# Two transformer blocks in float32 on one core: more tile pairs by seven block products, later waits, and subtractions moved from GpSimd to VectorE

## The reference

```python
def swiglu_ffn(h, w13, w2):
    g, u = jnp.split(h @ w13, 2, axis=-1)
    return (jax.nn.silu(g) * u) @ w2
```

## Time and profile before

| what | value |
|---|---|
| median of 3 runs | 1855.22 us (1853.93 to 1859.35) |
| the profiled execution's own time | 1851.81 us |
| its span in the profile | 1849.7 us |
| mean granted clock of TensorE | 0.996 of full speed |

### The profile page before, as it was taken

One profiled execution on the slowest core, in us unless ns is written; L12 is line 12 of the kernel. 1 busy time (PEld: TensorE's weight loads), 2 busy tenths in 40 slices (PEclk: granted clock), 3 DMA queues, 4 the chain that ended last, 5 costly groups with the idle time before them and its releaser, 6 DMA issues.

```text
span 1849.7 us, 28967 instructions
## 1 busy us (share of the span) xinstructions
PE 1811.9 (98%) x10711; PEld 1496.1 (81%) x10711; DVE 1076.8 (58%) x1548; ACT 764.8 (41%) x1137; POOL 217.5 (12%) x178
## 2 busy tenths in 40 slices
PE   7999999999999999999999999999999999999998
PEld 6787776788888888888879998788776879998787
DVE  6553686466777533444677777334666477776322
ACT  6635436454444322322443335223555353334322
POOL 0030001111111100000300003401000200003510
PEclk9999999999999999999999999999999999999999
DMA  6312112133333333333323333333220223333331
GB/s 192 82 37 58 47 47 69 46 92 99 94 101 92 94 94 100 100 96 98 95 88 102 91 102 99 94 94 105 77 77 1 80 81 101 102 91 105 90 104 66
DMA packets 309232, 161.08 MB, mean 87 GB/s; under 512 B 12688, under 2 KB 306832, under 8 KB 309024
## 3 DMA queue, kind: packets, MB, share of 16 engines
q1 hardware_dynamic: 308080, 157.28, 29.2%
q0 software_dynamic: 640, 2.17, 0.4%
q10 hardware_dynamic: 432, 0.52, 0.1%
HBM read 157.85 MB, written 2.10 MB: 86 GB/s over the span
## 4 chain that ended last, share of the span: by engine, by line
PE 91%; POOL 4%; DVE 2%; ACT 2%; issue 1%; DMA 0%; ACTq 0%; DVEq 0%
PE ps L382 27%; PE ps L384 27%; PE ps L383 27%; POOL h_hi L859 4%; PE ps L2116 1%; PE ps L1527 1%; PE ps L2433 1%; PE ps L2434 1%; PE ps L2107 1%; PE ps L1438 1%; PE ps L1844 1%; PE ps L1260 1%; PE ps L1788 1%; PE ps L1832 0%; PE ps L2213 0%
## 5 line engine op out<-in xcount | busy, mean ns | idle before, releaser
L382 PE MATMUL ps<-xhi,whi 128*128 128x512 f32 (+1 forms) x1512 | 584.5, 387 | 8.1 <-DVE t_lo L785 6.1
L383 PE MATMUL ps<-xlo,whi 128*128 128x512 f32 (+1 forms) x1512 | 575.4, 381 | 0.0
L384 PE MATMUL ps<-xhi,wlo 128*128 128x512 f32 (+1 forms) x1512 | 575.1, 380 | 0.0
L369 ACT ACTIVATE whi<-raw 128x1024 fp32r<-128x1024 f32 (+2 forms) x297 | 308.3, 1038 | 578.8 <-PE ps L384 578.3
L377 DVE TENSOR_TENSOR wlo<-raw,whi 128x1024 fp32r<-128x1024 f32 (+2 forms) x279 | 350.4, 1256 | 237.6 <-ACT whi L369 237.5
L382 PEld LDWEIGHTS ps<-xhi,whi 128*128 128x128 f32 x1512 | 285.4, 189 | 67.0 <-issue 11.3
L383 PEld LDWEIGHTS ps<-xlo,whi 128*128 128x128 f32 x1512 | 285.6, 189 | 54.9 <-issue 3.1
L384 PEld LDWEIGHTS ps<-xhi,wlo 128*128 128x128 f32 x1512 | 285.5, 189 | 54.6
L382 PE MATMUL ps<-h_lo,whi 128*128 128x512 f32 x352 | 137.4, 390 | 1.6 <-POOL h_hi L859 1.6
L384 PE MATMUL ps<-h_lo,wlo 128*128 128x512 f32 x352 | 137.0, 389 | 0.0
L383 PE MATMUL ps<-h_hi,whi 128*128 128x512 f32 x352 | 137.0, 389 | 0.0
(11 more groups left out here) (389 smaller groups left out, 2544.6 us busy)
## 6 DMA issues: line engine op xcount, KB each, us to landing
raw<-in_conv_ffn_w SPq DMA_DIRECT2D x52, 512.0 KB, 3.8
raw<-in_mla_ffn_w SPq DMA_DIRECT2D x52, 512.0 KB, 3.8
raw<-in_w_up SPq DMA_DIRECT2D x44, 512.0 KB, 3.8
raw<-in_w_in SPq DMA_DIRECT2D x28, 512.0 KB, 3.9
raw<-in_conv_w_in SPq DMA_DIRECT2D x24, 512.0 KB, 3.8
raw<-in_w_down SPq DMA_DIRECT2D x16, 448.0 KB, 3.4
raw<-in_conv_ffn_w SPq DMA_DIRECT2D x16, 448.0 KB, 3.4
raw<-in_mla_ffn_w SPq DMA_DIRECT2D x16, 448.0 KB, 3.4
```

What stands on the lines that cost most here:

```text
L369: a.activation(whi[:, u % PARTS, 0:n], raw[:, u % RAW, 0:n], ACT.Copy).then_inc(hi_split, 1)
L382: t_.matmul(out, wh, xh, start=first, stop=False)
L383: t_.matmul(out, wh, xl, start=False, stop=False)
L384: return t_.matmul(out, wl, xh, start=False, stop=last)
```

## The change

1. PATTERN becomes (False, True, True, False, True, True), six pairs a round and three rounds. Twelve of the 18 pairs in each loop are special instead of nine, and in each round there are two places where a special pair follows a special one.
2. `pe_seven` waits for single PSUM banks. Where the pair ahead is special too (`in_row`) it waits on `block_added`, the count of VectorE's adds in that pair: two adds before m1, six before m5, seven before m4. Otherwise it waits once, for the results of the pair before the one ahead.
3. The waits for the low parts of the four input sums move from ahead of the loop into each special pair, behind m1. On VectorE the low part of t4 is made one place earlier, ahead of the scaling of pair 2's up unit.
4. The low parts of the 22 gated tiles are made by VectorE (`dve_product_lo`) instead of GpSimd: four behind each of the last four units, six more at the end.

```diff
-PATTERN = (False, True)
+PATTERN = (False, True, True, False, True, True)
...
-        def pe_seven(pe, stage, u, i, s):
-            n0, b0 = TILE0[stage] + u, nth(stage, i, s, 4)
+        def pe_seven(pe, stage, u, i, s, in_row):
+            n0, a0 = TILE0[stage] + u - 2, nth(stage, i, s, 7) - 7
...
-            pe.wait_ge(acc_free, in_units(n0 + 1, i))
+            if in_row:
+                pe.wait_ge(block_added, a0 + 2)
+            else:
+                pe.wait_ge(acc_free, in_units(n0 + 2, i))
             pe.wait_ge(sums_lo, nth(stage, i, s, 2) + 2)
             multiply("m1", "g0", "x11").then_inc(block_done, 1)
+            for n in X_SUMS:
+                pe.wait_ge(*after(f"{stage} {n} lo"))
             multiply("m6", "s2", "t2")
             multiply("m2", "g1", "x21").then_inc(unit_used, 1)
-            pe.wait_ge(acc_free, in_units(n0 + 2, i))
+            if in_row:
+                pe.wait_ge(block_added, a0 + 6)
             multiply("m5", "s1", "t1").then_inc(block_done, 1)
...
+            if in_row:
+                pe.wait_ge(block_added, a0 + 7)
             multiply("m4", "u1", "t4").then_inc(unit_used, 1)
...
             pe_pair(pe, stage, 2, None, True)
-            for n in X_SUMS:
-                pe.wait_ge(*after(f"{stage} {n} lo"))
             with pe.Fori(0, ROUNDS) as i:
...
-        def pool_products_late(pool, stage, h, h_hi, h_lo):
-            for m in range(FT):
-                pool.wait_ge(prod_hi, PAIR0[stage] + m + 1)
-                g.tensor_tensor(h_lo[:, m, :], h[:, m, :], f32(h_hi[:, m, :]), ALU.subtract).then_inc(prod_lo, 1)
...
+        def dve_product_lo(dve, stage, m, h, h_hi, h_lo):
+            dve.wait_ge(prod_hi, PAIR0[stage] + m + 1)
+            v.tensor_tensor(h_lo[:, m, :], h[:, m, :], f32(h_hi[:, m, :]), ALU.subtract).then_inc(prod_lo, 1)
...
             dve_x_sum_lo(dve, stage, "t2")
+            dve_x_sum_lo(dve, stage, "t4")
             dve_up_unit(dve, stage, 2, None, 1, 1, zS)
             dve_product(dve, stage, 2, None, h, zS, yg)
-            dve_x_sum_lo(dve, stage, "t4")
...
                 if j:
                     dve_product(dve, stage, u + 2 * odd, None, h, zS, yg)
+                for m in range(4 * n, 4 * n + 4):
+                    dve_product_lo(dve, stage, m, h, h_hi, h_lo)
+            for m in range(16, FT):
+                dve_product_lo(dve, stage, m, h, h_hi, h_lo)
```

More of the change, by code:

```diff
@@ L745, in pe_up_seven @@
                     if special:
-                        pe_seven(pe, stage, 4 + 2 * n, i, sum(PATTERN[:n]))
+                        pe_seven(pe, stage, 4 + 2 * n, i, sum(PATTERN[:n]), PATTERN[n - 1])
                     else:
@@ L943, in dve_pair, with dve_up_seven @@
             dve_product(dve, stage, u, i, h, zS, yg)
-        def dve_up_seven(dve, stage, gain, rstd, h, zS, yg):
+        def dve_product_lo(dve, stage, m, h, h_hi, h_lo):
+            dve.wait_ge(prod_hi, PAIR0[stage] + m + 1)
+            v.tensor_tensor(h_lo[:, m, :], h[:, m, :], f32(h_hi[:, m, :]), ALU.subtract).then_inc(prod_lo, 1)
+        def dve_up_seven(dve, stage, gain, rstd, h, h_hi, h_lo, zS, yg):
             u0 = FIRST[stage]
@@ L2714, in _ @@
             pool_residual(pool, "conv_out", "conv norm sum full")
-            pool_products_late(pool, "ffn2_up", h, h_lo, h_hi)
             pool_residual(pool, "ffn2_down", "ffn2 norm sum full")
@@ L2718, in _ @@
             pool_residual(pool, "w_o", "mla norm sum full")
-            pool_products_late(pool, "ffn3_up", h, h_lo, h_hi)
             pool_residual(pool, "ffn3_down", "ffn3 norm sum full")
@@ L2971, in _ @@
             dve_residual(dve, "conv_out", False, "conv_ffn_norm_g_2")
-            dve_up_seven(dve, "ffn2_up", "conv_ffn_norm_g_2", "ffn2 norm rstd", h, zS3, yg3)
+            dve_up_seven(dve, "ffn2_up", "conv_ffn_norm_g_2", "ffn2 norm rstd", h, h_lo, h_hi, zS3, yg3)
             dve_residual(dve, "ffn2_down", True, "kv_norm_g_2")
@@ L2975, in _ @@
             dve_residual(dve, "w_o", False, None, "mla_ffn_norm_g_2")
-            dve_up_seven(dve, "ffn3_up", "mla_ffn_norm_g_2", "ffn3 norm rstd", h, zS3, yg3)
+            dve_up_seven(dve, "ffn3_up", "mla_ffn_norm_g_2", "ffn3 norm rstd", h, h_lo, h_hi, zS3, yg3)
             dve_residual(dve, "ffn3_down", True, None)
```

## The result

| | before | after |
|---|---|---|
| median, timed together | 1856.62 us | 1835.64 us (1833.57 to 1836.07) |
| ratio, with its 95% interval | | 0.9885 (0.9867 to 0.9903) |
| the same kernels timed together once more | 1853.16 us | 1835.97 us |
| ratio | | 0.9899 (0.9884 to 0.9914) |
| profiled execution's own time, its span | 1851.81, 1849.7 us | 1835.28, 1833.5 us |

The change makes the kernel faster by 1.0 to 1.2%. The ratio of the second measurement, on 1853.2 us, is 18.7 us less (15.9 to 21.5); that of the first, on 1856.6 us, is 21.4 us less. The forecast was 18.4 less and 1836.8 us.

What follows compares the result with a forecast made beforehand. TensorE was taken as the bound, with few gaps. Terms of -5.0 (pattern), -11.1 (input sums) and -2.3 us (low parts) make -18.4; from a median of 1855.2 that gives 1836.8 us, range 1831 to 1845.

Steps and rivals of the forecast that it cites:

- What bounds the kernel: Whole span: TensorE busy 98%, so time comes only from giving it less work or closing its few gaps.
- Part 1: Up loops: three more special pairs per stage, six in all at 0.84 us each, gain 5.0 us.
- Rival 5: Special pairs: 256-column matmuls cost half of 512-column ones, six pairs gain 8.3 instead of 5.0, 1833.5 us; chance 0.02.
- The seam: Where a special pair follows a special one, 12 places: VectorE's list is ready 0.25 us early, cost 0.
- Rival 1: Places where special follows special: each slips by 0.3 us, 3.6 us in all, 1840.4 us; chance 0.22.
- Part 2: TensorE's queue in special pairs: per-bank waits and extra waits are covered, cost 0, upper bound 6 us.
- Part 3: Head of both up loops: no wait for the input sums' low parts, 4.90 and 6.23 us, together 11.1 us gained.
- Part 4: Tails before the down stages: low parts on VectorE gain 2.9 less 0.6 us, net 2.3 us.
- Rival 2: Places where special follows special: VectorE becomes the bound, up to 2.7 us each, 32 us, 1869 us; chance 0.06.

Runs made afterwards that it cites:

- pattern alone: Kernel before with the new pattern and per-bank waits only; sums awaited ahead of the loop, t4 late, low parts on GpSimd: 1843.89 us, ratio 0.9959.
- one-more kernel: Changed kernel with one more 512-column VectorE product, read by nothing, ahead of the gate's low part at 12 places where special follows special: 1836.66 us, ratio 0.9912.
- the kernel with the waits put back: Changed kernel with the four waits for the input sums ahead of the loop again, t4's low part still early: 1836.49 us, ratio 0.9905.
- the filled pause: Kernel before with 13 matmuls into a free bank that nothing reads, behind pair 2 and ahead of the four waits: 1848.50 us, ratio 0.9973.
- low parts alone: Kernel before with VectorE instead of GpSimd making the low parts of the gated tiles: 1848.19 us, ratio 0.9981.

## Why the prediction was right

The forecast of 1836.8 us lies 0.8 to 1.2 above the two medians. That closeness is in part luck: it was set against a median of 1855.2 us for the kernel before, which was 1856.6 and 1853.2 when timed beside the change, and the gain of 18.4 us came out as 21.4 and 18.7. The account behind it is better judged by its parts.

- **What bounds the kernel** was right: only TensorE's work and its few gaps could give time, and GpSimd's 4% of the chain were worth 2.8 us in two tails, not 4%.
- **Part 1** (5.0 us): 2.58 a stage measured with the pattern alone, 5.2. The round came out at 31.06 for 31.05. The half sentence that "each matmul carries some 13 ns that do not shrink with its width" was right for this kernel and wrong as a statement on matmuls: the surcharge was 7 to 13 ns at 256 columns and 13 to 20 at 512, by where the operands lie. The Trainium skill (TensorE: Matmul & The Clock Gate, Back-to-back issue gap) gives 2.5 ns over the columns for isolated matmuls, by which the spacing would be 109 and 216 ns (an estimate from that page). No placement measured here gets there (113 to 120 and 227 to 233, in streams where each matmul has a weight load of its own), so the trace disagrees with that formula here. (By the prediction's own 10.36 and 9.17 us the six pairs would give 7.1, not 7.2.) Rival 5, which had almost no chance as a property of the width, turned out to be more than a third available (0.197 of 0.54 us a pair) by moving a tile.
- **The seam**: no cost, as forecast, but by two errors against each other. The low part ended 0.12 us later than laid out, and the restart that I subtracted (0.43, from the wait ahead of the loop) is 0.05 at a seam. The 0.43 was read rightly but belongs to that place, as it stays with a pause of 0.45 us and is absent at seams with a wait of 1.53. The slack was put at 0.25 and is 0.43 to 0.5. With 0.43 the one-more kernel would have lost some 0.5 per seam; it lost 0.18. Rival 1, at 0.22, was given too much for that reason. VectorE's share of the loop, laid out as 90%, was 86%.
- **Part 2** (0): confirmed by the kernel with the waits put back, for the four waits of each pair, and by the seams' 0.12.
- **Part 3** (11.1 us): 11.0 measured with this edit alone. Its split into pause and clock is confirmed by the filled pause (4.6 of 4.7 by the medians, 4.5 in the loops). But the clock's share varies like a draw: the same 3.0 us pause cost 1.7 us of slow clock in the first stage of three kernels (before, pattern alone, low parts alone), and 3.0, 0 and 1.6 in their second. Had the profile of before shown another of these, the term would have been 8 to 11; that it showed one that fits the medians was luck. The Trainium skill (TensorE: Matmul & The Clock Gate, Part 1: The HAM clock gate) says of the slow stretch at a kernel's start that its length varies from run to run of the same kernel. The traces show the like behind equal pauses, with 0.80, 0.89 and 1.00 of granted clock, but across kernels and stages; no kernel with the pause was profiled twice.
- **Part 4** (2.3 us): 2.76. The charge of 0.3 us a stage for the third down unit was not due. Its split ran from 1162.30 to 1163.39 and so ended 9.8 us behind the last scaling (9.9 laid out), and TensorE wanted it at 10.0. It was in time, TensorE shows no wait there, and so no restart was due.
- **Rival 2** was rightly set low for this pattern and is what happens one step further.

## What to carry to other kernels

When two edits aim at one gap, price the gap once, and count the slow clock behind the pause as part of it: here a wait of 3 us was worth 3.3 to 6.2 us, by how the clock fell, and either moving the producer or moving the wait would have done. When an engine with little total slack gets a list that must meet a deadline in its middle, lay the list out instruction by instruction up to that deadline and ask for how many repetitions the slack lasts; two in a row fitted by half a microsecond, three did not. Take the delay behind a wait from a wait at the same kind of place: 0.43 us ahead of the loop was 0.05 inside it. And before timing a variant that adds a tile, see that all later tiles keep their place: 64 bytes moved this kernel by 5 us down or 20 up, more than most of its edits.

## What the runs showed of the hardware

- The spacing of back-to-back float32r matmuls depends on where in memory the moving and the stationary tile start. With offsets in 128 bytes that differ by 64: 256 columns 0.114 to 0.118 us (0.1133 at the least), 512 columns 0.229 to 0.2333. With equal offsets: 256 columns 0.118 to 0.1200, 512 columns 0.2267. Only offsets of 0 and 64 were tried, and the offset alone does not fix the size.
- A restart of TensorE that waits for VectorE came 0.05 to 0.06 us behind it at the seams inside the loop, after 0.5 to 1.5 us without work, and 0.43 to 0.52 behind it at the wait ahead of the loop, after 0.45 to 3.1 us. The place decided, not the length of the pause; the reason is open.
- Equal pauses of 3.0 us left the granted clock of the 16 to 17 us from the hand-over on at 0.80, 0.89 or 1.00; with 13 matmuls in the pause it was 1.00 both times.

Not tried: 13 or 14 special pairs a stage, a pattern in which ScalarE or GpSimd takes over part of the sums, other offsets than 64 bytes, the better place of t together with one of the sums' edits alone, and another wait of TensorE at the head of a loop.
